# A fused block on one core: the last two column chunks of the MLA mixer's output product computed as a pair, with seven block products in place of eight

## The reference

```
return (o * jax.nn.silu(g)) @ w_out              # 256 x 2048 times 2048 x 2048
...
h = h + rms_norm(out, post_norm[i])
gate = jax.nn.sigmoid(rms_norm(h, ple_norm[i]) @ ple_w_gate[i])
h = h + (p[i] @ ple_w_proj[i]) * gate
```

## Time and profile before

| | us |
|---|---|
| median of three runs | 2442.62 (2442.57 to 2442.99) |
| profiled execution | 2443.45 |
| its span, first to last instruction | 2441.5 |
| PE busy | 2430.1 |
| DVE busy | 1689.0 |
| ACT busy | 1361.4 |
| POOL busy | 63.4 |

### The profile page before, as it was taken

How to read it: one execution, slowest core, us unless ns; L and a number is a source line. 1 busy time by engine, 2 the same in 40 slices (tenths; PEclk the granted TensorE clock), 3 DMA queues, 4 the chain that set the end, 5 groups by cost and what they waited for, 6 DMA issues and landing times.

```text
span 2441.5 us, 34053 instructions
## 1 busy us (share of the span) xinstructions
PE 2430.1 (100%) x12682; PEld 2087.7 (86%) x12682; DVE 1689.0 (69%) x2035; ACT 1361.4 (56%) x1804; POOL 63.4 (3%) x79
## 2 busy tenths in 40 slices
PE   9999999999999999999999999999999999999998
PEld 8888888887889999888888888888988888888886
DVE  7675757899765655656656767665666667679887
ACT  6444444556656655556755556555645545455555
POOL 0000000000100000010000000000000000000001
PEclk9999999999999999999999999999999999999999
DMA  8666666565555554555585554454565665656654
GB/s 313 198 189 186 186 189 187 183 222 183 190 177 180 178 156 140 208 209 190 169 231 165 161 176 144 164 181 155 174 189 181 189 189 181 190 169 206 219 186 142
DMA packets 234627, 453.03 MB, mean 186 GB/s; under 512 B 14961, under 2 KB 60449, under 8 KB 233356
## 3 DMA queue, kind: packets, MB, share of 16 engines
q1 hardware_dynamic: 230992, 435.94, 55.8%
q0 software_dynamic: 3120, 14.90, 1.7%
q10 hardware_dynamic: 396, 0.59, 0.2%
HBM read 448.68 MB, written 2.69 MB: 185 GB/s over the span
## 4 chain that ended last, share of the span: by engine, by line
PE 99%; DVE 1%; DMA 0%; ACT 0%; SPq 0%; issue 0%; ACTq 0%
PE ps L780 24%; PE ps L782 13%; PE ps L746 12%; PE ps L748 12%; PE ps L747 12%; PE ps L930 5%; PE ps L931 5%; PE ps L932 5%; PE ps L704 1%; PE ps L813 1%; PE ps L812 1%; PE ps L811 1%; PE ps L1382 1%; PE ps L1142 0%; PE ps L1154 0%; PE ps L1153 0%
## 5 line engine op out<-in xcount | busy, mean ns | idle before, releaser
L2354 DVE TENSOR_TENSOR w_lo<-raw,w_hi 128x1024 fp32r<-128x1024 f32 x702 | 860.8, 1233 | 505.7 <-ACT w_hi L1552 485.3
L1552 ACT ACTIVATE w_hi<-raw 128x1024 fp32r<-128x1024 f32 x702 | 740.2, 1060 | 678.1 <-PE ps L782 357.4
L780 PE MATMUL ps<-x_hi_lo,w_hi 128*128 128x512 f32 x2336 | 820.9, 394 | 0.6 <-DVE w_lo L2354 0.6
L782 PE MATMUL ps<-x_hi_lo,w_lo 128*128 128x256 f32 x2336 | 660.7, 283 | 0.0
L780 PEld LDWEIGHTS ps<-x_hi_lo,w_hi 128*128 128x128 f32 x2336 | 438.7, 188 | 102.0 <-DVE w_lo L2354 0.9
L746 PE MATMUL ps<-w_hi,x_hi_lo 128*128 128x512 f32 (+3 forms) x1248 | 487.2, 390 | 0.0
L748 PE MATMUL ps<-w_hi,x_hi_lo 128*128 128x512 f32 (+3 forms) x1248 | 478.9, 384 | 0.0
L747 PE MATMUL ps<-w_lo,x_hi_lo 128*128 128x512 f32 (+3 forms) x1248 | 477.9, 383 | 0.0
L782 PEld LDWEIGHTS ps<-x_hi_lo,w_lo 128*128 128x128 f32 x2336 | 439.2, 188 | 0.0
L1729 ACT ACTIVATE w_hi<-raw 128x1024 fp32r<-128x1024 f32 (+1 forms) x184 | 189.9, 1041 | 159.6 <-PE ps L932 143.7
L748 PEld LDWEIGHTS ps<-w_hi,x_hi_lo 128*128 128x128 f32 x1248 | 234.5, 188 | 42.1
(11 more groups left out here) (442 smaller groups left out, 2561.0 us busy)
## 6 DMA issues: line engine op xcount, KB each, us to landing
raw<-in_w_up SPq DMA_DIRECT2D x160, 512.0 KB, 4.4
raw<-in_pool_w_in SPq DMA_DIRECT2D x126, 512.0 KB, 4.0
raw<-in_w_in SPq DMA_DIRECT2D x96, 480.0 KB, 3.8
raw<-in_w_down SPq DMA_DIRECT2D x82, 512.0 KB, 5.3
raw<-in_pool_w_out SPq DMA_DIRECT2D x64, 512.0 KB, 4.8
raw<-in_ple_w_gate SPq DMA_DIRECT2D x64, 512.0 KB, 4.2
raw<-in_mla_w_in SPq DMA_DIRECT2D x56, 448.0 KB, 3.4
raw<-in_pool_w_group SPq DMA_DIRECT2D x32, 512.0 KB, 4.0
```

Source lines behind the costliest of these rows:

```text
L780: pe.matmul(bank, w_hi[:, slot, cols], xs[:, k].rearrange("p s n -> p (s n)"), start=k == 0, stop=False, skip_group_check=True)
L782: last = pe.matmul(bank[:, 0:T], w_lo[:, slot, cols], xs[:, k, 0, :], start=False, stop=k == nkt - 1, skip_group_check=True)
L1552: act.activation(w_hi[:, t.slot(), :], raw[:, slot, :], ACT.Copy).then_inc(S("w_hi"), 1)
L2354: dve.tensor_tensor(w_lo[:, t.slot(), :], raw[:, u % RAW, :], w_hi[:, t.slot(), :].bitcast(F32), ALU.subtract)\
```

## The change

The product keeps its chunks 0 and 1 plain. Chunks 2 and 3 become one pair with two quads, over the feature tiles 8 to 11 and 12 to 15; the tiles 0 to 7 stay plain. The product's features exist only as high and low parts, so the quads' sums of blocks start from the sum of the two parts, made on DVE during chunk 1 (`mixed_sums`). Since here all four blocks of sums are kept as tiles of their own, the block product that took a half of the features directly takes a sum. The four extra banks are those that the transposes use. Chunks 2 and 3 are read out by DVE (`quads_mixed`, `columns_out`) in place of ACT, and ACT squares them from `outt`; POOL's gain product of these two chunks waits for the squares.

```diff
+MLA_OUT_QUADS = [8, 12]
+M2, M3 = ([("plain", c, (k, k + 1)) for k in range(0, 8, 2)] for c in (2, 3))
+MQ = [[("quad", n, k)] for n, k in enumerate(MLA_OUT_QUADS)]
+MLA_OUT = [[], M2[:3] + MQ[0] + M3[:2] + MQ[1] + M2[3:] + M3[2:]]
...
     # SP
-        columns(w_mout)
+        for c in range(2):
+            chunk(w_mout, KT, c * 512)
+        paired(mla_out, w_mout)
...
     # PE, a quad
-                    block(e5, "e5", x.yh[:, y1, t1], x.yl[:, y1, t1], last)
+                    if x.both:
+                        block(e5, "e5", x.yh[:, y1, t1], x.yl[:, y1, t1], last)
+                    else:
+                        block(e5, "e5", x.sums_hi[3][:, q], x.sums_lo[:, 3, q], last)
...
     # PE, after the heads
-        for _ in range(NCH - 1):
-            chunk(xh, xl, KT)
+        chunk(xh, xl, KT)
+        heads_done(pe, "a")
+        paired(mla_out, "y_lo")
...
     # ACT
-        for c in range(NCH):
-            mixer_chunk(chunk(8) if c else out_first(), 6, c)
-            if c == 0:
-                split_p(1)
+        mixer_chunk(out_first(), 6, 0)
+        split_p(1)
+        hi(5)
+        act.wait_ge(S("y_done"), 2 * WB + 5)
+        act.activation(msums_hi, msums, ACT.Copy).then_inc(S("y_hi"), 1)
+        mixer_chunk(chunk(3), 6, 1)
+        for n, (kind, _, kts) in enumerate(MLA_OUT[1]):
+            if n >= LEAD:
+                step_hi(kind, kts)
+        hi(1)
+        t.add("chunk", 2)
+        square_mixed(2, "mla_out", 6)
+        hi(2)
+        square_mixed(3, "mla_out", 6)
...
     # DVE
+        def mixed_sums(n):
+            a21, a11, a12, a22 = range(4)
+            def block(m, j, tt):
+                hi_part, lo_part = (y[:, 8:16, tt * 128:tt * 128 + 128].rearrange("p (q j k) n -> p q j k n", q=2, j=2)[:, :, j].bitcast(F32)
+                                    for y in (xh, xl))
+                return dve.tensor_tensor(msums[:, m], hi_part, lo_part, ALU.add)
+            if n == 0:
+                heads_done(dve, "a")
+                dve.wait_ge(S("out_pair"), HEADS // 2)
+                block(a21, 0, 1)
+                block(a22, 1, 1)
+            elif n == 1:
+                block(a11, 0, 0)
+                step(block(a12, 1, 0))
+            elif n == 2:
+                stepped()
+                dve.tensor_tensor(msums[:, a22], msums[:, a21], msums[:, a22], ALU.add)
+                step(dve.tensor_tensor(msums[:, a21], msums[:, a11], msums[:, a21], ALU.subtract))
+            elif n == 3:
+                stepped()
+                step(dve.tensor_tensor(msums[:, a11], msums[:, a22], msums[:, a11], ALU.subtract))
+                stepped()
+                dve.tensor_tensor(msums[:, a12], msums[:, a12], msums[:, a11], ALU.subtract).then_inc(S("y_done"), 1)
+            else:
+                dve.wait_ge(S("y_hi"), len(POOL_Y) + 1)
+                dve.tensor_tensor(msums_lo, msums, msums_hi.bitcast(F32), ALU.subtract).then_inc(S("y_lo"), 1)
...
         split_p()
-        for c in range(1, NCH):
-            skip(8)
+        mixed_sums(0)
+        for n in range(1, 4):
+            lo(1)
+            mixed_sums(n)
+        lo(3)
+        mixed_sums(4)
+        lo(2)
+        t.add("chunk")
+        for n, (kind, _, kts) in enumerate(MLA_OUT[1]):
+            if n >= LEAD:
+                step_lo(kind, kts)
+            if n >= 8:
+                quads_mixed(1, n - 8, mla_out)
+        for n in (2, 3):
+            quads_mixed(1, n, mla_out)
+        lo(1)
+        columns_out(mla_out, outt, 2)
+        lo(2)
+        t.add("chunk", 2)
+        columns_out(mla_out, outt, 3)
...
     # POOL, before the gain product of a chunk
                     chunk_out(pool, "mla_out", c)
+                    if c >= 2:
+                        pool.wait_ge(S("squared_out"), NCH + c - 1)
```

More of the change, by code:

```diff
@@ L112 @@
 POOL_LOADS, POOL_RELEASED, POOL_QUADS_END, POOL_PLAIN_END = quad_tables(UNITS_END["pool"], POOL_OUT, 0)
-DOWN_LOADS, DOWN_RELEASED, DOWN_QUADS_END, DOWN_PLAIN_END = quad_tables(UNITS_END["up"], DOWN, SINCE_POOL_OUT)
+SINCE_MLA_OUT = SINCE_POOL_OUT + 3 * len(MLA_OUT_QUADS)
+MLA_OUT_PAIR = UNITS_END["heads"] + 16
+MLA_OUT_LOADS, MLA_OUT_RELEASED, MLA_OUT_QUADS_END, MLA_OUT_PLAIN_END = quad_tables(MLA_OUT_PAIR, MLA_OUT, SINCE_POOL_OUT)
+DOWN_LOADS, DOWN_RELEASED, DOWN_QUADS_END, DOWN_PLAIN_END = quad_tables(UNITS_END["up"], DOWN, SINCE_MLA_OUT)
 RELEASED = list(range(UNITS_END["pool"])) + POOL_RELEASED
-RELEASED += range(UNITS_END["pool_out"] + SINCE_POOL_OUT, UNITS_END["up"] + SINCE_POOL_OUT)
+RELEASED += range(UNITS_END["pool_out"] + SINCE_POOL_OUT, MLA_OUT_PAIR + SINCE_POOL_OUT)
+RELEASED += MLA_OUT_RELEASED
+RELEASED += range(UNITS_END["mla_out"] + SINCE_MLA_OUT, UNITS_END["up"] + SINCE_MLA_OUT)
 RELEASED += DOWN_RELEASED
-ALL_PRODUCTS = TOTAL_UNITS + SINCE_POOL_OUT + 3 * 2 * len(DOWN_QUADS)
-assert len(RELEASED) == TOTAL_UNITS and len(POOL_LOADS) == 64 and len(DOWN_LOADS) == 90
+ALL_PRODUCTS = TOTAL_UNITS + SINCE_MLA_OUT + 3 * 2 * len(DOWN_QUADS)
+assert len(RELEASED) == TOTAL_UNITS and len(POOL_LOADS) == 64 and len(MLA_OUT_LOADS) == 16 and len(DOWN_LOADS) == 90
+assert all(r <= UNITS_END["mla_out"] + SINCE_MLA_OUT - RAW + n for n, r in enumerate(MLA_OUT_RELEASED[-RAW:]))
 assert POOL_RELEASED[-RAW:] == [UNITS_END["pool_out"] + SINCE_POOL_OUT - RAW + n for n in range(RAW)]
@@ L431, in build, with __init__ @@
     class Paired:
-        def __init__(self, name, y, yh, yl, tiles, sums, sums_hi, sums_lo, quads, steps, loads, quads_end, plain_end, before):
+        def __init__(self, name, y, yh, yl, tiles, sums, sums_hi, sums_lo, quads, steps, loads, quads_end, plain_end, pairs_before):
             self.name, self.y, self.yh, self.yl, self.tiles = name, y, yh, yl, tiles
             self.sums, self.sums_hi, self.sums_lo, self.quads = sums, sums_hi, sums_lo, quads
-            self.steps, self.loads, self.quads_end, self.plain_end, self.before = steps, loads, quads_end, plain_end, before
+            self.steps, self.loads, self.quads_end, self.plain_end, self.pairs_before = steps, loads, quads_end, plain_end, pairs_before
+            self.both = len(steps[0]) > 0
         def first_chunk(self):
@@ L445, in bank @@
         def bank(self, c, tt):
-            return ps[:, 4 * (c // 2) + 2 * self.set_of(c) + tt, :]
+            return ps[:, (4 * (c // 2) if self.both else 0) + 2 * self.set_of(c) + tt, :]
         def quad_banks(self, p):
-            return [ps[:, 4 * (1 - p) + n, :] for n in range(4)]
+            return [ps[:, (4 * (1 - p) if self.both else 4) + n, :] for n in range(4)]
         def blocks(self, j, tt):
@@ L464, in build @@
     down = Paired("down", fy, fyh, fyl, DOWN_Y, fsums, fsums_hi, fsums_lo, DOWN_QUADS, DOWN, DOWN_LOADS,
-                  DOWN_QUADS_END, DOWN_PLAIN_END, SINCE_POOL_OUT)
+                  DOWN_QUADS_END, DOWN_PLAIN_END, 3)
+    msums, msums_lo, msums_hi = (arena(f"mla_y_sums{n}", off, [128, 4, len(MLA_OUT_QUADS), 2, 128], dt)
+                                 for n, off, dt in (("", 81920, F32), ("_lo", 81920, F32R), ("_hi", 90112, F32R)))
+    mla_out = Paired("mla_out", None, xh, xl, [], msums, [msums_hi[:, m] for m in range(4)], msums_lo, MLA_OUT_QUADS, MLA_OUT,
+                     MLA_OUT_LOADS, MLA_OUT_QUADS_END, MLA_OUT_PLAIN_END, 1)
     ps = ctx.enter_context(nc.psum_tensor("ps", [128, 8, 512], F32))[:]
@@ L505, in build, with since @@
     OUT_PIECES = [("gained", 0), ("added", 1024), ("gained", 512), ("added", 1536)]
+    def since(linear):
+        if linear == "pool":
+            return 0
+        return SINCE_POOL_OUT if UNITS_END[linear] < UNITS_END["mla_out"] else SINCE_MLA_OUT
     def products(eng, linear, more=0):
-        eng.wait_ge(S("w_used"), UNITS_END[linear] + RING + more + (0 if linear == "pool" else SINCE_POOL_OUT))
+        eng.wait_ge(S("w_used"), UNITS_END[linear] + RING + more + since(linear))
     def evacuated(eng, linear):
@@ L625, in paired @@
                 t.add("unit")
-            t.add("more", 6 * len(x.quads))
+            t.add("more", 3 * len(x.quads) * (2 if x.both else 1))
         paired(pool_out, w_pout)
@@ L932, in times, with paired @@
             return pe.matmul(dst, yl_, wh, start=False, stop=final)
-        def paired(x, split, pairs_read, ending=()):
+        def paired(x, split, ending=()):
             def pair(p):
@@ L1013, in pair @@
                     pe.wait_ge(S(f"mm_free{s}"), t.at(f"set{s}", 1))
-                else:
-                    pe.wait_ge(S("quads_read"), pairs_read + 1)
+                elif x.both:
+                    pe.wait_ge(S("quads_read"), x.pairs_before + 1)
+                else:
+                    s = x.set_of(2)
+                    pe.wait_ge(S(f"mm_free{s}"), t.at(f"set{s}", 1))
                 steps = x.steps[p][:-len(ending)] if p == 1 and ending else x.steps[p]
@@ L1023, in pair @@
                     else:
-                        if c == 0 and p == 0:
+                        if c == 0 and not x.both:
```

(10 more changed lines are left out.)

20 lines of the change are left out of this document (13 added, 7 removed).

## The result

The changed kernel takes 2447.46 us (median of 20 runs, 2446.35 to 2449.86) against 2442.84 for the kernel before beside it: a ratio of 1.0019, 95% interval [1.0012, 1.0025], 4.6 us slower. Run again later beside another set it took 2447.38 against 2443.04, 1.0018 [1.0009, 1.0027], 4.3 us. The prediction was 2446.6, 4.0 us slower, in a range of 2442.8 to 2448.8.

A forecast was written before the change was run, and what follows sets the result against it. TensorE, busy in all of the span, was taken to bound the kernel. Matmuls saved, front, first quad and tail summed as -2.79 + 0.4 + 1.2 + 5.15 = +3.96 us, giving a median of 2446.6, range 2442.8 to 2448.8.

The forecast's parts named there:

- What is taken away: TensorE's queue in both quads: 12 fewer matmuls at 0.2323 us each, 2.79 us saved at most.
- The front: Chunk 1: two adds ahead of the fourth unit's low part make it late; 0 to 1.05 us, taken as 0.4.
- The first quad: Low parts of blocks 3 and 5 late behind POOL's gain product of chunk 1; two stops, 1.2 us with restarts.
- The second quad: VectorE has its sixth block ready at 31.2, TensorE wants it at 31.9; cost 0, at most 0.7 us.
- The tail: After the second quad: chunk 3's late evacuation delays the second and third ple units; 5.15 us, bounds 3.75 and 5.5.
- The loads: Fetches of 16 units, a quad's holding slots longer; slots return 5 us or more before next use, nothing added.
- The sum: Whole kernel: -2.79 + 0.4 + 1.2 + 5.15 = +3.96 us, a median of 2446.6.
- faster rival: Tail: chunk 3's evacuation is not late, the tail is free and all 2.79 us remain; 2439.8, chance 0.07.
- the second rival: Second in the prediction's list: chunk 3's evacuation on time in the tail, 2439.8 us; chance 0.07.
- first rival: POOL does not get in VectorE's way: front 0, first quad 0, tail 3.75, sum +0.96, 2443.6; chance 0.18.

The follow-up runs named there:

- the first experiment: Changed kernel with the tail reordered: ScalarE's three high parts before squaring chunk 2, one VectorE low part after evacuating chunk 3; 2442.43 us, ratio 0.9999.
- the front's experiment: Changed kernel with the low part of chunk 1's fourth unit put ahead of VectorE's first two adds; 2446.24 us, ratio 1.0014.
- the fourth: Changed kernel with POOL's gain product of chunk 2 also waiting for the squares of chunk 3; 2448.07 us, ratio 1.0021.
- the third experiment: Changed kernel with POOL's gain products of chunks 0 and 1 delayed until the sums are made and the quads' banks read; 2445.38 us, ratio 1.001.
- all at once: Changed kernel with tail and front reordered and POOL's product of chunk 1 held until the second quad's extra banks are read; 2441.16 us, ratio 0.9992.

## Why the prediction was right

**What is taken away.** Right: 12 matmuls, which shorten the stretch without stops by 2.8 us, and with nearly all stops removed the time falls by what is left of 2.79.

**The front** was under-sized, 0.4 taken and 1.02 measured. The prediction let POOL hold up one add, or both, or none, and chose near the middle. The first add, which by its record began 0.6 us ahead of POOL's product, was held until POOL's pair was over and took 3.74 us; the second came after it in its usual 0.68. So both stood behind the whole pair, the upper of its bounds (1.05).

**The first quad** came out as counted, stops ahead of blocks 3 and 5, 1.20 against 1.2 us. It started from 1.49 and 2.31 for the two instructions that POOL met, the durations of the earlier trace rows, and taking POOL away took both stops away. The count itself is a little off: the times that the prediction gives (12.98 against 12.56, 16.40 against 15.91) leave 0.42 and 0.49, not 0.46 and 0.53, so its own sum is 1.1. **The second quad** has none.

**The tail** is 4.89 against 5.15. With the second quad's end at T = 1078.0 (VectorE's copy starts at 1078.18 after 0.16 idle), the steps foretold and measured: evacuation of chunk 2 at T + 5.8 and 5.7, high part at 8.75 and 8.65, POOL at 8.7 and 8.7, second low part done at 13.5 and 13.3, second ple unit at 14.8 and 14.5, third at 19.0 and 18.7. Of the 0.3 us, 0.1 is there before POOL starts; the rest is POOL's pair, which took 3.51 us beside two low parts that together took 3.51. The halves of the pair and the low parts end in turn, 1.1 us apart, where the prediction counted 1.25 for a half and 1.14 for a low part.

**The loads**, at which the prediction put nothing, stand nowhere on the chain of waits between 1011 and 1104 us.

**The sum.** By stops it is +4.3 where 3.96 was foretold. That it came so near is in part luck: the front was 0.62 too low and the tail 0.26 too high. Of the 0.9 us between the median and 2446.6, these make 0.4, the kernel before ran 0.2 slower beside it than the 2442.62 that the prediction starts from, and 0.3 is unexplained.

Where a reader might have gone wrong: the tail's price is not a price of VectorE's added work. The prediction named the order as the cause and the first experiment removed nearly all of the 4.9 us with the same instructions (0.34 came back ahead of the gate product). Its faster rival (the evacuation on time, 2439.8) described what the experiments then built, and 2441.16 is 1.4 us above that figure: 0.9 is the stop behind the turns of `h`, and 0.4 is the kernel before, which ran at 2443.04 beside it and not at 2442.62.

The exclusion on which all three places rest agrees with the Trainium skill, SBUF — State Buffer, section "Who interferes with whom": a VectorE instruction with two SBUF inputs contends with a GpSimd one that reads SBUF, and one with at most one SBUF input, outside the two-port modes, does not. The rows show both: an add, a difference and a low part beside POOL take 3.74, 2.31 and 1.79 us where 0.68 and 1.22 are usual, while the evacuation at 1082.04, one of whose inputs lies in PSUM, keeps its 1.27 us for two with POOL busy from 1081.13 on. One instruction with a single SBUF input waits all the same, the mean on 128x2 elements:

```profile
1094.35 1.12 DVE L2537 TENSOR_SCALAR mean_square<-mean_square 128x2 f32<-128x2 f32 x1
```

It takes 0.17 us in the ten places of this trace where no product of POOL runs; here it ends at 1095.47, 0.03 us after the first half of POOL's pair. In which mode it runs no row shows. The kernel before has the same (1.08 us at 1090.70), so it is no part of the difference. Which engine goes first is not settled by the starts in these rows: the add of 3.74 us began 0.6 us ahead of POOL's pair and waited for all of it, while in the first quad and in the tail the two engines took turns.

One slip of the prediction bears on this. It says that without the exclusion the sum would be the second rival's; what it describes is its first rival, 2443.6.

## What to carry to other kernels

Moving a read-out from one engine to another moves it into that engine's written order: look at what is written ahead of it, and at what that waits for, before counting the engine's load. Where the saved work is 0.1% of a full queue, stops of half a microsecond decide; count the arrival of each tile against its due time rather than busy shares. A product of POOL pushed out of one collision is still to be done, and lands on later two-input work of VectorE; whether that work has time to spare decides what it costs.

## What the runs showed of the hardware

TensorE's granted clock fell after the long stop in some executions, to the lower of its two levels (1.2 of 2.4 GHz), and not in others. In the repeat of the changed kernel, TensorE ran without a break for 29 us until its stop of 3.2 us, and then:

```profile
1093.02 0.71 PE L772 MATMUL ps<-w_hi,ple_hi 128*128 128x512 f32 x1 [3.21 <-DVE mixer_out L2461]
...
1093.96 0.63 PE L774 MATMUL ps<-w_hi,ple_lo 128*128 128x512 f32 x1
1094.39 0.63 PE L772 MATMUL ps<-w_hi,ple_hi 128*128 128x512 f32 x1
```

The window over it (busy times with counts, then the granted clock, DMA share and GB/s):

```profile
1093.90:1097.00 3.10, 3.10 (x9) 2.38 (x8) 2.00 (x4) 2.86 (x6) 2.33 (x2) 0.57 0.32 114
```

Matmuls start 0.43 us apart in place of 0.23 up to 1096.52, at a mean clock of 0.57 over the window; from 1096.78 on they are back at 0.23. The same was seen in the front's experiment (0.53) and after the shorter stop of 2.1 us in the fourth; in the first profile of the changed kernel and in the third experiment, with the same stop of 3.2 us, the clock stayed at 1.00. It cost little here: from the second ple unit to the first turns 7.25 us with it, 7.11 without, because the third ple unit would have waited for the root anyway. Without that cover nine matmuls at 0.43 would cost some 1.8 us, an estimate from these rows. In the kernel before and in the two versions without a long stop (the tail's order, all at once) the granted clock of every run listed is 0.999; in the changed kernel it is 0.997 to 0.999. Whether that makes its wider scatter was not settled: 2449.86 us came at 0.997, but 2448.48 at 0.999.
